# Context tiles score their latent heads one map at a time, with their own output-piece table, a far chunk's product one step later, and step 2's first transposes ahead of a late projection

## What is computed

```python
for l in range(DEPTH):
    want_ctx = l < DEPTH - 1
    mod = jax.nn.silu(c) @ w_mod[l] + b_mod[l]
    u = split_cols(h @ w_in[l]);  uc = split_cols(hc @ w_in[l])
    a_lat, a_ctx = gqa_mixer(...)
    b_lat, b_ctx = na_mixer(...)
    c_lat, c_ctx_out = diff_mixer(...)
    d_lat, d_ctx = mla_mixer(...)
    x = x + g1 * (jnp.concatenate([a_lat, b_lat, c_lat, d_lat], axis=-1) @ w_out[l])
    x = x + g2 * moe_ffn(h2, ...)

def mla_mixer(...):                       # the latent heads
    qx = jnp.concatenate([q_nope, q_pe], axis=-1)     # 64 + 32
    kx = jnp.concatenate([k_nope, jnp.broadcast_to(k_pe, ...)], axis=-1)
    if want_ctx:
        out_ctx = attend(qcx, ((kcx, vcx),), scale)

def attend(q, kvs, scale):
    s = jnp.einsum('bqhgd,bkhd->bhgqk', q, k)
    p = jax.nn.softmax(s * scale, axis=-1)
    out = out + jnp.einsum('bhgqk,bkhd->bqhgd', p, v)
```

## Time and profile before

| | us |
|---|---|
| median of 3 runs | 1527.3 (1526.41 to 1528.31) |
| the profiled execution | 1524.59 |
| its span, first to last instruction | 1522.8 |
| PE busy | 1466.7 (96%) |
| DVE busy | 795.7 (52%) |
| ACT busy | 393.7 (26%) |
| POOL busy | 307.6 (20%) |

### The profile page before, as it was taken

The page is one execution under the profiler, slowest core; times in us unless marked ns, Lnnn a source line. Parts: engine busy times, 40 slices in busy tenths (PEclk is TensorE's granted clock), DMA queues, the critical chain, the costliest instruction groups (busy, mean ns, idle before and its releaser), DMA issues.

```text
span 1522.8 us, 25197 instructions
## 1 busy us (share of the span) xinstructions
PE 1466.7 (96%) x9490; PEld 968.2 (64%) x9490; DVE 795.7 (52%) x1768; ACT 393.7 (26%) x895; POOL 307.6 (20%) x457
## 2 busy tenths in 40 slices
PE   5999999999999999999999999999999999999995
PEld 4655445666665568688787554556666666788883
DVE  2333533467676645664554753524667764753335
ACT  1322113445554420000000422113455541000001
POOL 0111101000000000365553121210000000365532
PEclk9999999999999999999999999999999999999998
DMA  9642113640011177699998743214811026589994
GB/s 357 210 165 111 56 38 94 210 166 15 29 42 42 43 288 268 256 331 361 354 364 334 281 177 141 76 53 128 274 53 43 15 94 213 197 322 335 342 357 173
DMA packets 104698, 282.01 MB, mean 185 GB/s; under 512 B 20036, under 2 KB 34156, under 8 KB 95096
## 3 DMA queue, kind: packets, MB, share of 16 engines
q1 hardware_dynamic: 91824, 259.52, 47.8%
q0 software_dynamic: 12192, 21.02, 3.7%
q10 hardware_dynamic: 584, 0.14, 0.0%
HBM read 259.44 MB, written 38.01 MB: 195 GB/s over the span
## 4 chain that ended last, share of the span: by engine, by line
PE 91%; DMA 3%; DVE 2%; issue 2%; ACT 1%; POOL 1%; SPq 0%; DVEq 0%; POOLq 0%; ACTq 0%
PE S L1346 18%; PE S L1742 17%; PE B L1525 9%; PE S L1753 8%; PE PT L1466 6%; PE B L1502 6%; PE S L1445 4%; PE B L1370 3%; DMA arena<-in_w_mod 2%; PE B L1242 2%; PE S L1370 2%; PE S L1435 2%; PE S L1423 2%; PE S L1609 1%; PE S L1616 1%
## 5 line engine op out<-in xcount | busy, mean ns | idle before, releaser
L1346 PE MATMUL S<-arena 128*128 128x512 f32 (+3 forms) x768 | 296.0, 535 | 2.8 <-ACT arena L1004 2.8
L1742 PEld LDWEIGHTS S<-arena 128*128 128x128 f32 x2240 | 257.2, 193 | 18.5 <-issue 18.5
L1742 PE MATMUL S<-arena 128*128 128x128 f32 x2240 | 257.8, 276 | 1.7 <-issue 1.7
L1346 PEld LDWEIGHTS S<-arena 128*128 128x128 f32 x768 | 139.8, 190 | 123.2 <-issue 102.1
L1114 ACT ACTIVATE arena<-S,nmax 128x768 f32<-128x768 f32 (+1 forms) x200 | 154.6, 777 | 150.0 <-DVE nmax L2260 80.3
L1920 POOL DMA_INDIRECT arena<-h,arena x140 | 150.4, 1075 | 161.2 <-DVEq L2558 102.3
L1525 PE MATMUL B<-arena 128*128 128x512 f32 x320 | 155.9, 604 | 0.6 <-DVE arena L2320 0.5
L1466 PEld LDWEIGHTS PT<-cst,arena 128*128 128x128 f32 x768 | 86.4, 141 | 79.0 <-issue 57.1
L1753 PE MATMUL S<-arena 128*128 128x512 f32 x280 | 126.0, 592 | 0.0
L1466 PE MATMUL PT<-cst,arena 128*128 128x128 f32 x768 | 114.1, 278 | 8.0 <-issue 4.9
L1502 PEld LDWEIGHTS B<-arena 128*64 128x64 f32 x1536 | 83.0, 136 | 36.5 <-issue 31.2
(11 more groups left out here) (332 smaller groups left out, 1735.9 us busy)
## 6 DMA issues: line engine op xcount, KB each, us to landing
arena<-in_w_mod SPq DMA_DIRECT2D x24, 2048.0 KB, 11.1
arena<-in_moe_w_gate SPq DMA_DIRECT2D x35, 1024.0 KB
arena<-in_moe_w_up SPq DMA_DIRECT2D x35, 1024.0 KB
arena<-in_moe_w_down SPq DMA_DIRECT2D x35, 1024.0 KB
arena<-in_w_in SPq DMA_DIRECT2D x6, 2048.0 KB, 11.3
arena<-y SPq DMA_DIRECT2D x20, 512.0 KB, 5.6
arena<-mod SPq DMA_DIRECT2D x16, 512.0 KB, 6.8
arena<-in_tokens SPq DMA_DIRECT2D x12, 512.0 KB, 9.7
```

The costliest lines, as they stand in the source:

```text
L1346: mm = pe.matmul(ubank[u % 4][:, c0:PANEL_W[p]], hT[:, k, t * P:(t + 1) * P], panel[p][:, k, c0:], start=k == 0, stop=k == KT - 1)
L1742: mm = pe.matmul(to, wgu[b][:, w, k * DE + h * P:k * DE + (h + 1) * P], XT[b][:, k, :], start=k == 0, stop=k == KT - 1)
```

## The change

Four things are changed, all in what PE's program says; the other engines' programs read the same table of far chunks and are otherwise as they were.

1. `score` for a latent-head step of a context tile (four steps in all: k = 5 and 9 of tiles 4 and 5) writes map 0's 64-row part and its rotary part, signals `scored`, and then does the same for map 1. The first map waits for one exponential less of the step before.
2. Context tiles take a table of their own, `CTX_PIECES`, for the sixteen pieces of the tile before.
3. Far chunk 10 is multiplied in step 8 in place of step 7, in both layers.
4. In each step the projections (`nb_unit`) come behind `product(.., 0)`. The two meet in one step only, step 2 of tile 0, in both layers.

```diff
-FAR_STEPS = {4: 8, 6: 9, 7: 10, 9: 11}
+FAR_STEPS = {4: 8, 6: 9, 8: 10, 9: 11}
 PIECES = {0: (0, 1), 1: (1, 2), 2: (2, 5), 3: (5, 6), 4: (6, 8), 5: (8, 10), 6: (10, 12), 7: (12, 13), 8: (13, 14), 9: (14, 16)}
+CTX_PIECES = {0: (0, 2), 1: (2, 3), 2: (3, 5), 3: (5, 6), 4: (6, 8), 6: (8, 11), 7: (11, 12), 8: (12, 14), 9: (14, 16)}
                     if n:
-                        pe.wait_ge(s["exp_done"], 2 * n)
+                        pe.wait_ge(s["exp_done"], 2 * n - int(kind == "m" and t >= TL))
                     if kind == "m":
-                        parts = [(0, HALF, 0), (HALF, NTOK, 512)] if t < TL else [(SEQ, NTOK, 0)]
+                        if t >= TL:
+                            for m in range(2):
+                                if m:
+                                    pe.wait_ge(s["exp_done"], 2 * n)
+                                rows, ks, qs = maps[m]
+                                turned = slice(64 * m, 64 * m + 32)
+                                pe.matmul((S0, S1)[m][:, 0:CTX], qk[rows, qs, cols], qk[rows, ks, SEQ:NTOK], start=True, stop=False)
+                                pe.matmul((S0, S1)[m][:, 0:CTX], qk[turned, SL_MQ + 2 + i, cols], qk[turned, SL_MK + 2, SEQ:NTOK], start=False, stop=True).then_inc(s["scored"], 1)
+                            return
+                        parts = [(0, HALF, 0), (HALF, NTOK, 512)]
-                    in_step = PIECES if t < nt else LAST_PIECES
+                    in_step = LAST_PIECES if t == nt else PIECES if t < TL else CTX_PIECES
                     if t < nt:
                         score(t, k)
-                    for nb in nb_units_in(l, n):
-                        nb_unit(nb)
                     two = after and STEPS[kp][0] != "d"
                     if two and n < NS:
                         product(tp, kp, 0)
+                    for nb in nb_units_in(l, n):
+                        nb_unit(nb)
```

## The result

| | before | changed |
|---|---|---|
| median of the timed runs, us | 1528.28 (1523.34 to 1531.02, 19 runs) | 1532.17 (1528.38 to 1541.72, 19 runs) |
| the profiled execution: time, span | 1524.59, 1522.8 | 1528.38, 1526.5 |

The ratio is 1.0036, with a 95% interval of 1.0024 to 1.0047: slower by 0.36% (the medians alone stand 3.9 us apart, 0.25%). 1529.6 was forecast, 2.3 us above the 1527.3 of three runs, and the measured median lies 0.4 us above the range. Before's own median beside this result is 1.0 us above those 1527.3.

A forecast was written before the change was run, and what follows sets the result against it. PE, busy 96% of the span, was taken as the bound. Terms -2.2 + 0 + 0 + 5.05 - 0.6 = +2.3 us on 1527.3 gave 1529.6 us, range 1525.0 to 1531.8.

The forecast's parts named there:

- sizing of the map-by-map scores: Context tiles' four latent steps: height changes make four groups run one by one, 2.52 us against 1.26; +5.05 us.
- (a): Context tiles' latent scores: starts in order, no emptying, three groups, 1.89 us; sum -0.3, 1527.0 us; chance 16%.
- (b): Context tiles' latent scores stay side by side at 1.26 us, step 6 waits 0.8 twice; sum -1.8, 1525.5 us; chance 13%.
- rival (c): Layer 0: clock falls behind PE's 2.8 us idling before chunk 11, costing 1.7 us more; 1531.3 us; chance 10%.
- Step 2's transposes: Tile 0, both layers: moved ahead of the projection, the 1.10 us wait before the second transposes goes; -2.2 us.
- Chunk 10, layer 0: Tile 0: the 2.39 us weight wait goes, but PE waits 2.8 us before chunk 11 instead; net 0.
- Chunk 10, layer 1: Tile 0: new 0.6 us wait before step 8's scores, while the chunk fills step 8's 0.51 us wait; net 0.
- The context tiles' pieces: Tiles 4 and 5: waits before steps 9 and 2 shrink, new 0.3 us wait before step 6, twice; -0.6 us.

The follow-up runs named there:

- crossed order: Changed kernel with latent score products ordered map 0's 64 rows, map 1's 32, map 0's 32, map 1's 64; 1525.11 us, one execution.
- maps_only: Kernel before with only the map-by-map latent scores in context tiles; 1536.57 us, ratio 1.0050 to before.
- changed_again: The changed kernel, unaltered, timed and profiled a second time; 1530.77 us against 1528.47 for before, ratio 1.0011.
- one_height: Changed kernel, still map by map, with rotary parts read from 64 rows instead of 32; 1545.74 us, whole execution, with other expert work.
- pairs_back: Changed kernel with context tiles' latent scores side by side as before, other three edits kept; 1524.26 us against 1529.12 for before, ratio 0.9961.
- pairs_twice: Changed kernel with context tiles' latent scores made side by side and made twice over; 1530.0 us, ratio 1.0005 to before.
- tile0_only: Kernel before with only step 2's transposes moved ahead of the projection and far chunk 10 in step 8; 1526.43 us, ratio 0.9988.
- far_only: Kernel before with only far chunk 10 moved to step 8; 1528.98 us against 1528.47 for before, ratio 1.0002.
- chunk11_first: Changed kernel with side-by-side scores, step 5's two pieces back, layer 0's chunk 11 weights issued ahead of half the output weights; 1523.09 us, ratio 0.9962 to before.
- transposes_only: Kernel before with only step 2's first transposes moved ahead of the projection, chunk 10 in step 7; 1527.01 us, ratio 0.9990.

## Why the prediction was wrong

**The failed step is the sizing of the map-by-map scores at +5.05 us, the one term that decided the sign.** It took two groups more a step, priced them at the full clock, and took those 5.05 as the upper bound, with no reason given why nothing should come on top. Its mechanism held: 2.50 us a step for 2.52, and rivals (a) and (b) fell (1.89 needs a crossed order, 1.27 the old one). Missing was what the order does to the clock: profiles with map-by-map scores show two falls in the context tiles (changed, maps_only) or none (changed_again), and none of the eight other profiles, before's among them, shows one there, leaving out one_height, whose groups were 1.07 us. Two falls are 3.4 us. By the mean granted clock the changed kernel loses about 3.5 us an execution against before, and maps_only, which has these scores alone, 1.8; so the size is known to a factor of two.

The forecast with 3.5 more is +5.8 us. Measured were +3.9 by the medians and +5.5 by the ratio. Of the distance between the forecast time and the measured one, 2.6 us, 1.0 is the base: before took 1528.28 beside the result, not 1527.3.

I had weighed a clock fall, but as rival (c), behind an idle wait, because the only fall that I had looked at stood behind 1.65 us of idling. PE is never idle in the 3.4 us ahead of the fall at 503.30.

**Point by point.**

- Step 2's transposes: -1.10 forecast in each layer, -1.34 and -1.33 measured. The bracket goes as forecast. The other 0.23 stand in no bracket, but in the distances from row to row: the projection takes 6.86 us to the next row instead of 6.97, the first six transposes 0.72 instead of 0.81, and the second six 0.66 instead of 0.69.
- Chunk 10, layer 0: the wait went over to chunk 11 as forecast (2.8), with 2.28 to 3.81 us in the profiles, since the transfer's end varies. Net 0 holds where the clock does: +0.22 in changed_again, -1.08 in the first profile.
- Chunk 10, layer 1: a new wait of 0.6 forecast, 0.54 measured; net -0.27 by the rows of the last projection and of tile 1's first piece (0 forecast).
- Rival (c), given 10%, is real: behind waits of 3.4 to 3.8 us the clock fell in pairs_back, pairs_twice, tile0_only and far_only, and held in changed_again and, behind 3.38 us, in one_height. It costs tile 0 about 1.7 us where it comes. Neither profile of the changed kernel has it, and pairs_back, whose profile has it, is faster than before; how often it comes in the timed runs of the changed kernel isn't known.
- The context tiles' scores: +5.05 forecast, +4.94 by changed_again's rows.
- The context tiles' pieces: -0.6 forecast. In changed_again the tiles are 3.23 us longer in all, so the pieces gave -1.7. The brackets explain 1.19 of it. Three waits of 1.26 us in sum are gone, and two new ones of 0.16 came (0.3 each forecast; the prediction's own terms, 0.12 + 0.45 + 0.56, end at 492.09 and make it 0.23). A fourth wait that went is one that the prediction didn't list: 0.24 us ahead of the second transposes of tile 4's step 0, which the second piece of that step in `CTX_PIECES` now fills. Before, then changed_again:

```profile
473.26 0.85 PE L1466 MATMUL PT<-cst,arena 128*128 128x128 f32 x6 [0.24 <-issue]
```
```profile
472.70 0.82 PE L1477 MATMUL PT<-cst,arena 128*128 128x128 f32 x6
```

- The other 0.5 of the pieces stands in distances from row to row: 0.27 in those of the pieces, 0.14 in those of the statistics products and 0.09 in those of the transposes. With side-by-side scores it is the same: pairs_back's -0.64 is 0.12 in brackets and 0.52 in distances.
- At full clock the sum therefore was too high: by changed_again's rows -2.7, +0.2, -0.3 and +3.2 make +0.4, for +2.3 forecast. That the forecast came as near as it did is in part luck: an error of 1.9 us, most of it in the pieces, covered part of the missing 3.5. The two profiled spans differ by 2.9 us and not by 0.4; 1.7 of that is the fall near 1326 us, where no edit reaches, twice as long as before's.

**What stays open.** Why one execution has the falls and the next does not. That half of the array stands empty in turn is the likely cause and is not proven. Pairs_twice differs from the changed kernel in that, and also in doing twice the work in that time, in the wait between the maps and in the signals; these were not separated, beyond that one_height has the same wait and signals and no fall in its one profile, with groups of 1.07 us. Falls in the context tiles stand in two of the three profiles with map-by-map scores and changing height, and in none of the other nine, which is few of each. The timed runs have a mean clock but no stretches, so that their extra falls lie in the context tiles is inferred from the profiles, and the split of their 3.2 us into clock and length is an estimate from means. The profile with the falls and the one without are one each of the changed kernel.

## What to carry over

In these runs two products shared the array only while all that was in flight had the same row height: group parts by height, all 64-row parts and then all 32-row parts, even when each map could be signalled sooner on its own. When an order leaves half of the array empty, look at the granted clock as well as at the length, and look also where the engine is never idle. When a wait for weights is filled, ask what stands behind it on the same queue and reorder the queue (chunk11_first), or the wait goes to the next transfer. Before a difference in mean clock is put down to one place, list the falls of the whole execution: some stand where no edit reaches.

## What the hardware did that I had not expected

- The granted clock fell to 0.50 for 3.4 us behind stretches in which PE was hardly ever idle: busy for 3.40 of the 3.40 us ahead of the fall at 503.3 and for 3.24 ahead of 527.2 in the changed kernel, for 3.28 ahead of 506.1 and 3.18 ahead of 543.6 in maps_only, each time within 4 us after map-by-map scores began.
- It held at 1.00 behind 3.57 us of idling in changed_again and fell behind 2.40 us in transposes_only: the length of the wait alone does not decide it.
- The change of height empties the whole array, also between halves that share nothing: 1.89 us for the crossed order against 1.26, while with one height the four products took 1.07, map by map.
